# Retention of prompt tiles 3 to 5 moved into the second group's front, and the choice of a later group's first tile dealt first

## What is computed

```python
h = rms_norm(x, norm1_g)
rq, rk, rv, rg, fq, fk, fv, logf = project(h, ...)      # h @ w_in, 7 blocks of 512 columns and 8 forget columns
ro, s_new = retention(rotary(rq), rotary(rk), rv, s0)   # 8 heads of 64, decaying state carried from chunk to chunk
fo = fox(fq, fk, fv, logf, past)                        # 8 heads of 64, attention with forget bias
x = x + concat(rms(ro) * silu(rg), rms(fo)) @ w_out
# PEER, for each token (128 x 128 = 16384 experts, 8 heads, 16 of each)
q = rms_norm(x, norm2_g) @ wq
s1, s2 = q[:, :, 0] @ keys[0], q[:, :, 1] @ keys[1]
v1, i1 = top_k(s1, 16);  v2, i2 = top_k(s2, 16)
cv, ci = top_k(v1 + v2 (all pairs), 16);  e = i1 * 128 + i2
g = softmax(cv);  w = g * gelu(x . u[e])
x = x + sum over heads and k of w * v[e]
```

## Time and profile before

| | us |
|---|---|
| median of 3 runs | 3725.55 |
| lowest, highest | 3722.57, 3727.93 |
| the profiled execution's span | 3730.6 |
| PE busy | 2358.7 (63%) |
| DVE busy | 2458.9 (66%) |
| ACT busy | 492.7 (13%) |
| POOL busy | 1431.5 (38%) |
| bytes moved | 1350.24 MB, of them 1208.03 MB by the gathers |

### The profile page before, as it was taken

The page is one execution under the profiler, slowest core; times in us unless marked ns, Lnnn a source line. Parts: engine busy times, 40 slices in busy tenths (PEclk is TensorE's granted clock), DMA queues, the critical chain, the costliest instruction groups (busy, mean ns, idle before and its releaser), DMA issues.

```text
span 3730.6 us, 32224 instructions
## 1 busy us (share of the span) xinstructions
PE 2358.7 (63%) x10549; PEld 927.0 (25%) x10549; DVE 2458.9 (66%) x6363; ACT 492.7 (13%) x1368; POOL 1431.5 (38%) x1276
## 2 busy tenths in 40 slices
PE   7999888886666777763765767774343343334333
PEld 4454443332233233220332332331000000000000
DVE  3263247888666578888855665788887565565655
ACT  2011321112222111011201221110111000000000
POOL 1011003563445343444333444344444444444443
PEclk9999899898788899876666788986565656566656
DMA  3024528999999999999999999999999999999999
GB/s 142 2 52 139 195 89 350 391 396 418 413 415 419 421 397 413 413 387 397 417 388 402 404 415 411 405 410 413 418 409 417 418 418 418 415 420 420 419 419 372
DMA packets 226726, 1350.24 MB, mean 362 GB/s; under 512 B 33840, under 2 KB 53176, under 8 KB 75904
## 3 DMA queue, kind: packets, MB, share of 16 engines
q0 software_dynamic: 165888, 1208.03, 78.6%
q1 hardware_dynamic: 60384, 139.57, 10.2%
q10 hardware_dynamic: 288, 0.59, 0.0%
HBM read 1322.73 MB, written 25.37 MB: 361 GB/s over the span
## 4 chain that ended last, share of the span: by engine, by line
DMA 34%; PE 21%; DVE 17%; POOL 9%; issue 7%; ACT 1%; POOLq 0%; DVEq 0%; ACTq 0%
DMA M<-in_peer_uv,M 34%; PE yp L2391 12%; POOL M L1842 8%; DVE M L2748 7%; PE ab L2339 2%; PE d L2138 1%; PE ab L2103 1%; DVE exg L2765 1%; DVE strips L2770 1%; PE ef L2373 1%; DVE M L2446 1%; DVE M L2531 1%; DVE M L2527 1%; PE d L2318 1%; PE c L2318 1%
## 5 line engine op out<-in xcount | busy, mean ns | idle before, releaser
L1842 POOL DMA_INDIRECT M<-in_peer_uv,M x1152 | 1326.8, 1152 | 1767.9 <-PE yp L2391 1429.6
L2748 DVE SCALAR_TENSOR_TENSOR M<-M 128x1024 f32<-128x1024 f32 x1152 | 1408.6, 1225 | 770.7 <-DMA M<-in_peer_uv,M 737.7
L2391 PE MATMUL yp<-M,strips 128*32 128x512 f32 x4608 | 878.5, 903 | 1129.5 <-DVE strips L2770 1087.8
L2391 PEld LDWEIGHTS yp<-M,strips 128*32 128x32 f32 x4608 | 157.3, 144 | 1720.2 <-DVE strips L2770 1331.2
L2055 ACT ACTIVATE gel<-gel 128x4 f32<-128x4 f32 x288 | 59.1, 205 | 1968.7 <-DVE gel L2759 1947.6
L2339 PE MATMUL ab<-M 128*128 128x512 f32 x576 | 263.8, 607 | 5.3 <-ACT M L2009 5.3
L433 PE MATMUL z<-M 128*128 128x512 f32 x368 | 162.2, 597 | 0.9 <-PEq L105 0.9
L2339 PEld LDWEIGHTS ab<-M 128*128 128x128 f32 x576 | 108.3, 195 | 143.6 <-issue 137.9
L2217 PE MATMUL ab<-M 128*128 128x512 f32 x288 | 135.6, 624 | 10.9 <-DVEq L2557 10.9
L2770 DVE SCALAR_TENSOR_TENSOR strips<-gel,exg 128x128 f32<-128x128 f32 x288 | 84.0, 292 | 31.8 <-ACT gel L2055 22.4
L2576 DVE CUSTOM_DVE_ANT_0 M<-ab,M 128x896 f32<-128x896 f32 (+6 forms) x64 | 48.4, 756 | 85.5 <-PE ab L2104 70.7
(11 more groups left out here) (309 smaller groups left out, 2575.1 us busy)
## 6 DMA issues: line engine op xcount, KB each, us to landing
M<-in_c_win SPq DMA_DIRECT2D x13, 2048.0 KB, 10.3
M<-in_c_wq SPq DMA_DIRECT2D x12, 2048.0 KB, 11.4
M<-in_peer_uv,M POOLq DMA_INDIRECT x1152
M<-in_w_out SPq DMA_DIRECT2D x24, 512.0 KB, 8.0
M<-in_x_prompt SPq DMA_DIRECT2D x16, 512.0 KB, 11.6
x_scratch<-M SPq DMA_DIRECT2D x9, 512.0 KB, 7.9
M<-x_scratch SPq DMA_DIRECT2D x9, 512.0 KB
M<-hts_scratch SPq DMA_DIRECT2D x8, 512.0 KB, 13.0
```

Of the source, the lines that this page charges most:

```text
L1842: nc.gpsimd.indirect_dma_start(ring[n % NR], None, a["peer_uv"], bass.IndirectOffsetOnAxis(ap=idxH[:, t % 6, s // 4, s % 4:s % 4 + 1], axis=0)
L2391: last = nc.tensor.matmul(yp[32 * j:32 * j + 32, 512 * c:512 * c + 512], strips[:, n % 2, j, :], ring[(4 * n + j) % NR][:, D + 512 * c:D + ...
L2748: nc.vector.scalar_tensor_tensor(out=row, in0=row, scalar=1.0, in1=xrep[:, s % 4, :], op0=ALU.mult, op1=ALU.mult, accum_out=dots[:, t % 2, ...
```

## The change

Retention of tiles 3, 4 and 5 leaves the head. `AFTER` becomes 3 to 7, and `EARLY` 0, 1, 2 and 8. In the head the queries, keys, values and retention steps of the three tiles go. The sample state's four pieces are now made in the two steps that are left behind tile 8, two in each; the second `add_state` of a step stands behind the gated norm.

`retain` runs once for each of the groups 1 and 2. In group 1 it stands behind `project` and ahead of attention: twelve projections (four blocks by three tiles), with the same four weight blocks loaded again, three tiles of h, the running state read from and written back to memory, the gains, and the rest of the step for three tiles. The loads of K, V and Q of group 1 wait for its last step. The retention rows of tiles 3 to 5 are no longer stored in the head and loaded in the tail; they go straight to `mix`.

In `deal`, when the next step of `choice` is of a later group's first tile (3 or 6), `choice` is looked at first, so that it wins a tie.

```diff
-        AFTER = [6, 7]
+        RETAINED = {1: [3, 4, 5], 2: [6, 7]}
+        AFTER = [t for late in RETAINED.values() for t in late]
...
-            PIECE = {ORDER[2 + r]: r for r in range(PAIRS)}
+            PIECE = {ORDER[2]: (0, 1), ORDER[3]: (2, 3)}
...
                     if t in PIECE:
-                        state_sample(PIECE[t])
+                        state_sample(PIECE[t][0])
                     for k in range(LEAD if t == ST else 0 if whole else KC - 1, KC):
                         gate(t, k)
+                    if t in PIECE:
+                        state_sample(PIECE[t][1])
...
                     if t in PIECE:
-                        add_state(PIECE[t])
-                    if s + 1 < STEPS and ORDER[s + 1] in PIECE:
-                        spread(PIECE[ORDER[s + 1]])
+                        add_state(PIECE[t][0])
+                        spread(PIECE[t][1])
+                    elif s + 1 < STEPS and ORDER[s + 1] in PIECE:
+                        spread(PIECE[ORDER[s + 1]][0])
                     gated(t)
+                    if t in PIECE:
+                        add_state(PIECE[t][1])
+                        if s + 1 < STEPS:
+                            spread(PIECE[ORDER[s + 1]][0])
...
+                NL = len(RETAINED[g])
                 n, NJ = 4 * GT, 4 * NL
-                add(rest, ("lload", g, 0), sp=(bulk((2.1, 16)), ("pe", ("rq", g - 1, 2 * GT - 1, 1))))
...
+                if g == 1:
+                    before = [("pe", ("pmm", 0, PJ - 1, 1)), ("pe", ("pmm", 0, 2 * LATE - 1, 1))]
+                    clear = [*routed, ("act", ("rmove", 0, GT - 1))]
...
+                if g in RETAINED:
+                    retain(g, routed)
+                    last = len(RETAINED[g]) - 1
+                    routed = [("dve", ("lret", g, last)), ("dve", ("lup", g, last))]
...
+            def by_need(e):
+                i = at[e][1]
+                if i < len(queue[e][1]):
+                    _, g, t = queue[e][1][i][0][:3]
+                    if g and t == 0:
+                        return 1, 0
+                return 0, 1
...
-                    for th in range(len(threads)):
+                    for th in by_need(e):
...
+                            i0 = len(RETAINED[g])
+                            if i0 < GT:
+                                sp.dma_start(mix[:, i0:, 0:GW], a["rets"][t0 + i0:t0 + GT].rearrange("t p c -> p t c")
+                                             ).then_inc(mix_in, 16)
```

More of the change, by code:

```diff
@@ L649, in _ @@
                     sp.dma_start(a["rets"][t], mixo[:, t, 0:GW]).then_inc(out_done, 16)
[L650 to L651 removed]
+                    for r in PIECE.get(t, ()):
                         sp.wait_ge(sn_out, r + 1)
@@ L932, in emit @@
         PAIRED = 84
-        LATE, NL = TILES - GT, len(AFTER)
+        LATE = TILES - GT
+        NKEPT = {g: sum(len(RETAINED[x]) for x in RETAINED if x < g) for g in RETAINED}
         PJ = 3 * LATE
```

263 lines of the change are left out of this document (141 added, 122 removed).

## The result

In eight executions of each, the changed kernel took 3761.4 us in the median and the kernel before 3734.5: a ratio of 1.0076, with a 95% interval of 1.0059 to 1.0094. The change makes the kernel 0.8% slower, some 28 us. The forecast was 3735 against 3725.6, 9 us slower, with a range that ended at 3754. The direction was right, the size was a third of what came, and the time lies outside the range. Of the 26 us between the forecast and the measured time, 9 are the base: the forecast started from 3725.6, the median of three executions, and over eight, those three among them, the kernel before takes 3734.5. The other 18 or so are an error about the change itself.

The account below looks back on a forecast made before the run. A head bound by PE and DVE, then a tail bound by the full DMA queue: 3730.6 - 91.6 (head) + 24.2 (bytes) + 76.4 (pause) = 3739.6, 9.0 above; 3725.6 + 9.0 = 3735 us, range 3712 to 3754.

Parts of the forecast that it names:

- The head: Part before the first gather, where PE and DVE prepare group 0: three tiles shorter, 91.6 us sooner.
- The bytes: Tail of gathers: 10.1 MB more through a full DMA queue at 418 GB/s, 24.2 us.
- the bytes are free: Rival on the tail: the new loads slip into room in the queue, 24 us come off, 3711; chance 12%.
- The pause: Row 384, tile 3's first gather: no gather can be issued until tile 3's late choice ends; net 76.4 us.
- T: End of product 383 on DVE, from which the pause was timed; set at 1672.2 us.
- the lower bound: Least net pause at row 384, 62 us, if all four weight blocks fit into it.
- Work put beside the gathers: nothing: Rows of tile 1: about 124 us more for PE and 49 for DVE, costed at nothing.
- a ring of 22 us: Nine gathers in the tail, 2.5 us each, taken to cover the work put beside them.
- The tail's rate: GB/s of the gathers: 418 with gathers alone, 411 in the mean; added bytes were costed at 418.
- The priority: Choice of group 1's first tile dealt ahead of other steps: takes one top-sixteen step, 5.8 us, out of the pause.
- PE holds the gathers up as well: Rival on the tail: late weight loads make PE stand before strips the ring needs, costing 20 us, 3755; chance 15%.
- No pause: Rival at row 384: tile 3's choice comes in time all the same, 3659; chance 4%.

Follow-up runs that it names:

- allowances: Changed kernel with later groups' steps dealt 8 us further ahead on PE and DVE, 1.0279; with attention steps alone 6 us ahead, 1.0138.
- traces with two tiles: Changed kernel with only tiles 4 and 5 in group 1's front: 1.0008; also with attention dealt 6 us ahead, 1.0081, or smaller assumed projection cost, 1.0033.

## Why the prediction was right, and where it failed

- **The head: right.** 91.6 us predicted, 92.4 in the pair of traces it was worked out for, 90.0 over all; each phase within 1.4.
- **The bytes: right.** 10.1 MB and 24.2 us predicted, 10.3 and 25.0 found. The rival "the bytes are free" is out: seven eighths of the weights taken away gave 16 us. The rate in the last stretch is 418 again.
- **The pause: right, in size and mechanism.** 76.4 us net predicted, 75.5 found. Within it two errors cancel. T came late: a weight block issued at 1582.9 stood between the last gathers, product 382 waited 4.8 us for its gather, and by product 383 PE had already done the replication, so that strip 95 ended at T + 3.1 for 7.6. That made the part behind T 4.7 us shorter, and the idle time began ahead of T. And product 384 came 9.1 us behind its gather for 5.7, since DVE, in its order, still had a top-sixteen step, the gate and a turn to do. One sum of the term was off and decided nothing: with two more weight blocks in the pause, 9.8 MB, the lower bound is 66 and not 62.
- **"Work put beside the gathers: nothing": wrong.** This is one step that failed. I had set the cover, a ring of 22 us, against steps of 7 and stopped there. The retention's rows 96 to 192 have 10.6 us of idle queue that they had not, in all three traces. Shortening the moved projections took 5.7 of them away, in the rows where these stand; the rest, ahead of them, stays open.
- **The tail's rate, taken as unchanged: wrong by 10.3 us.** This is the other. 409.0 GB/s for 410.4 while the queue runs. Rows 416 to 544 carry about half of it (403 for 409 and 410), and there it goes with the priority: 410.0 in the changed kernel without it, 401 in the kernel before with it. Part of that is a shift between rows, since the whole tail without the priority still runs at 409.4. The rest, spread over the tail, stays open.
- **The priority: wrong in size.** Worth 15 us in the pause and not 5.8. That changed nothing in the sum, which rested on the order with the priority in it. That the priority also costs something, 15 us where there is no pause to shorten, was in no term.
- **The rivals.** "PE holds the gathers up as well" was right in kind: it had 3755. It named late weight loads and the clock; the loads' size is not it and the clock was 1.00; whether the loads came late was not tested. At 15% its 3755 lay one us outside the range. "No pause" is out.

Together: 3739.6 was the sum, 3759.9 came, 20.3 more. The two terms set at nothing make 20.9; the other errors, none over 4 us, cancel, which is luck. The range had reached for one of them at most, since I had made the rivals exclude each other, where small losses from a fuller PE and a fuller queue come together.

## What to carry to other kernels

Work taken from a serial head and put beside a full DMA queue was not free here: it paid its bytes at the queue's rate, and it moved everything behind it in the same in-order streams towards the next point that must be met. Look for that point first, count what stands in the order between the last product of one tile and the first gather of the next, and look at the next such border too. And a front that is late can't be dealt sooner at will: allowances that shortened or removed the pause cost more than it elsewhere, in the one kind with DVE at 90%, in the other with both engines below 70%, where PE standing in front of a step whose inputs were not there is the likely reason, not a tested one.

## What was not expected of the hardware

In one of the traces with two tiles, gather 0 goes at 506.0 us; in the two other kernels with the same head at 478.8 and 478.5. The 27 us stand in group 0's attention. Stretches of that trace, then of one of the others:

```profile
320.00:340.00 20.00, 14.75 (x49) 6.12 (x50) 2.34 (x11) 5.48 (x16) 0.00 (x0) 0.73 0.52 154
340.00:400.00 60.00, 58.95 (x178) 29.78 (x178) 9.03 (x40) 19.63 (x68) 0.00 (x0) 0.50 0.42 139
```
```profile
320.00:340.00 20.00, 15.49 (x63) 6.89 (x63) 2.89 (x14) 6.50 (x21) 0.00 (x0) 0.83 0.54 148
340.00:380.00 40.00, 35.84 (x188) 19.42 (x188) 9.66 (x41) 20.77 (x74) 0.00 (x0) 1.00 0.56 208
```

The granted clock of TensorE is 0.50, its lower level of 1.2 GHz, for 60 us on end, with PE busy for 58.95 of them; before it fell, PE had worked 14.75 of 20 us, against 15.49 where it did not fall. In that state the work of 40 us takes over 60. Where PE is the bound, as in this head, a single execution was so 27 us off, about the size of the whole effect studied here. In the tail, where the queue is the bound, the rate was 418 GB/s at a clock of 0.60: there a low clock costs nothing that shows.
